# Second mixer: attention score products over all 128 rows, with half-zero keys, in place of 64 rows each

## The reference, cut to what matters

```python
def chunked_relpos_attention(q, k, v, q_gain, k_gain, rel_bias):
    q = rms_norm_2(q, q_gain)
    k = rms_norm_2(k, k_gain)
    ...
    s = jnp.einsum('bnqhd,bnkhd->bhnqk', qc, kb).astype(jnp.float32) * (HEAD_DIM ** -0.5)
    ...
    s = jnp.where(valid[None, None, :, None, :], s + bias[None, :, None], NEG_INF)
```

## Time and profile before

| | us |
|---|---|
| median of three runs | 2283.86 |
| span of the profiled execution, first to last instruction | 2283.2 |
| around the span (median less span) | 0.66 |
| TensorE matmul busy | 2079.1 (91%) |
| TensorE weight loads busy | 1764.9 (77%) |
| VectorE busy | 1232.4 (54%) |
| ScalarE busy | 854.6 (37%) |
| GpSimd busy | 498.0 (22%) |
| second mixer's attention steps 0 to 31 | 1705.5 to 1850.7 |

### The profile page before, as it was taken

How to read it: one execution, slowest core, us unless ns; L and a number is a source line. 1 busy time by engine, 2 the same in 40 slices (tenths; PEclk the granted TensorE clock), 3 DMA queues, 4 the chain that set the end, 5 groups by cost and what they waited for, 6 DMA issues and landing times. The chain is left out here.

```text
span 2283.2 us, 30308 instructions
## 1 busy us (share of the span) xinstructions
PE 2079.1 (91%) x11592; PEld 1764.9 (77%) x11592; DVE 1232.4 (54%) x2338; ACT 854.6 (37%) x1402; POOL 498.0 (22%) x339
## 2 busy tenths in 40 slices
PE   6988898899999999798989999998799999789984
PEld 6887777788888788786768888887797778777773
DVE  3676453544454447745554544448952233478885
ACT  4444433421222344343332222224224452257772
POOL 2654321000000146432110000004453335110001
PEclk9999988999999999898989999999899999799997
DMA  4111100412221111110132212207445533489995
GB/s 154 56 56 38 37 29 19 175 64 102 110 110 55 42 57 56 38 38 28 38 120 111 101 65 110 110 1 178 63 128 175 153 128 121 151 320 401 406 391 211
DMA packets 61627, 270.95 MB, mean 119 GB/s; under 512 B 15040, under 2 KB 19904, under 8 KB 37056
## 3 DMA queue, kind: packets, MB, share of 16 engines
q1 hardware_dynamic: 52864, 237.84, 30.0%
q10 hardware_dynamic: 6048, 22.02, 2.5%
q0 software_dynamic: 2592, 9.44, 1.1%
HBM read 244.14 MB, written 37.19 MB: 123 GB/s over the span
## 5 line engine op out<-in xcount | busy, mean ns | idle before, releaser
L1241 PE MATMUL fill_ps<-w_hi,h_hi 128*128 128x256 f32 (+1 forms) x704 | 214.2, 304 | 13.9 <-ACT values L866 5.2
L1241 PE MATMUL fill_ps<-w_hi,h_lo 128*128 128x256 f32 (+1 forms) x704 | 204.7, 291 | 0.0
L1241 PE MATMUL fill_ps<-w_lo,h_hi 128*128 128x256 f32 (+1 forms) x704 | 204.2, 290 | 0.0
L795 POOL TENSOR_TENSOR w_lo<-w_raw,w_hi 128x1024 fp32r<-128x1024 f32 x60 | 151.8, 2540 | 194.3 <-ACT w_hi L858 193.6
L516 DVE TENSOR_TENSOR ffn_silu<-ffn_silu,ffn_up 128x512 f32<-128x512 f32 x44 | 30.2, 687 | 285.5 <-ACT ffn_silu L474 285.5
L322 POOL TENSOR_SCALAR norm_ss<-norm_ss 128x1 f32<-128x1 f32 x24 | 4.9, 203 | 798.8 <-ACT ffn_raw_d L316 738.2
L1241 PEld LDWEIGHTS fill_ps<-w_hi,h_hi 128*128 128x128 f32 x704 | 141.8, 201 | 27.0 <-issue 16.1
L1702 POOL TENSOR_TENSOR w_lo<-w_raw,w_hi 128x1024 fp32r<-128x1024 f32 x48 | 126.1, 2643 | 165.2 <-ACT w_hi L1787 165.2
L528 DVE TENSOR_TENSOR x<-ffn_down,x 128x512 f32<-128x512 f32 x176 | 119.1, 689 | 71.2 <-PE ffn_down L590 70.4
L1321 PEld LDWEIGHTS o_ps<-values,prob_t 128*128 128x128 f32 x800 | 111.6, 201 | 57.5 <-DVE prob_t L1100 46.3
L575 PE MATMUL ffn_up<-h_hi,w_hi 128*128 128x512 f32 x384 | 152.1, 396 | 3.7 <-PEq L772 3.7
(11 more groups left out here) (444 smaller groups left out, 5639.6 us busy)
## 6 DMA issues: line engine op xcount, KB each, us to landing
moe_raw_gu<-in_w_e_gu SPq DMA_DIRECT2D x46, 1024.0 KB, 11.9
w_raw<-in_w_mix SPq DMA_DIRECT2D x28, 1024.0 KB, 4.9
w_raw<-in_w_two SPq DMA_DIRECT2D x23, 1024.0 KB, 5.0
moe_raw_d<-in_w_e_down SPq DMA_DIRECT2D x23, 1024.0 KB, 8.3
w_raw<-in_w_gate SPq DMA_DIRECT2D x22, 1024.0 KB, 5.6
w_raw<-in_w_up SPq DMA_DIRECT2D x22, 1024.0 KB, 6.5
ffn_raw_d<-in_w_down SPq DMA_DIRECT2D x22, 1024.0 KB, 4.9
moe_in<-in_zero SPq DMA_DIRECT2D x23, 512.0 KB, 7.5
```

What stands on the lines that cost most here:

```text
L795: nc.gpsimd.tensor_tensor(w_lo[s][:, cols], w_raw[s][:, cols], w_hi[s][:, cols].bitcast(F32), ALU.subtract).then_inc(lo_done, 1)
L1241: last = nc.tensor.matmul(b[:, 0:cols], aw[:, k, t * P:(t + 1) * P], ww[:, k, 0:cols], start=k == 0 and n == 0, stop=k == KD - 1 and n == 2)
```

## The change

Score products take all 128 partitions. The queries of both heads of a pair are then the stationary operand, so the keys must be zero where the other head lies. For an even head the key unit itself gets zeros on partitions 64 to 127: its buffer is zeroed (`memset`, for units 1 and 3), and later only partitions 0 to 63 are written. For an odd head GpSimd makes a separate pair of tiles, `odd_keys`: the turned keys multiplied by a column `odd_row` that is 0 on partitions 0 to 63 and 1 on 64 to 127 (three operations on 128x512 for each pair of heads, in `keys_of_odd`). They stand in GpSimd's queue behind unit 1 and at the start of steps 8, 16 and 24. The space comes from the unused half of `rel_bias`. Three semaphores are added.

```diff
+        odd_row = core.sb("odd_row", [P, 1], ctx=st)
-        rel_bias = core.sb("rel_bias", [P, 4 * SEQ], ctx=st)
+        rel_bias = core.sb("rel_bias", [P, 2 * SEQ], ctx=st)
+        odd_buf = core.sb("odd_keys", [P, 2 * SEQ], F32R, st)
...
                     s = u % 4
-                    nc.gpsimd.tensor_copy(u_hi[s], unit_in[u % 2]).then_inc(unit_hi, 1)
+                    if u in (1, 3):
+                        nc.gpsimd.memset(units[s].bitcast(F32), 0.0).then_inc(padded, 1)
+                        pool.wait_ge(padded, 2 + (u + 1) // 2)
+                    rows = EVEN if u % 2 else slice(0, P)
+                    nc.gpsimd.tensor_copy(u_hi[s][rows], unit_in[u % 2][rows]).then_inc(unit_hi, 1)
                     pool.wait_ge(unit_hi, u + 1)
-                    nc.gpsimd.tensor_tensor(u_lo[s], unit_in[u % 2], u_hi[s].bitcast(F32), ALU.subtract).then_inc(unit_lo, 1)
+                    nc.gpsimd.tensor_tensor(u_lo[s][rows], unit_in[u % 2][rows], u_hi[s][rows].bitcast(F32), ALU.subtract).then_inc(unit_lo, 1)
+
+                def keys_of_odd(m):
+                    if m:
+                        pool.wait_ge(scored, 2 * TB * m)
+                    else:
+                        pool.wait_ge(padded, 3)
+                    hi, lo, src = odd_keys[0], odd_keys[1], unit_in[1]
+                    nc.gpsimd.tensor_scalar(hi, src, odd_row[:], None, ALU.mult).then_inc(odd_hi, 1)
+                    pool.wait_ge(odd_hi, 2 * m + 1)
+                    nc.gpsimd.tensor_tensor(lo, src, hi.bitcast(F32), ALU.subtract).then_inc(odd_hi, 1)
+                    pool.wait_ge(odd_hi, 2 * m + 2)
+                    nc.gpsimd.tensor_scalar(lo, lo.bitcast(F32), odd_row[:], None, ALU.mult).then_inc(odd_lo, 1)
...
+                nc.gpsimd.memset(odd_row[:], 1.0).then_inc(padded, 1)
+                pool.wait_ge(padded, 1)
+                nc.gpsimd.memset(odd_row[EVEN], 0.0).then_inc(padded, 1)
...
                 unit(0)
                 unit(1)
+                keys_of_odd(0)
...
                 for n in range(REL_LAST + 1):
+                    if n % (2 * TB) == 0 and 0 < n < REL_STEPS:
+                        keys_of_odd(n // (2 * TB))
...
                     if u >= 2:
                         act.wait_ge(unit_lo, u - 1)
+                        if u % 2:
+                            act.wait_ge(odd_lo, u // 2)
...
                     qs, ks = a // 2 * 2 % 4, (a // 2 * 2 + 1) % 4
-                    width, cols, rows = (i + 1) * P, slice(i * P, (i + 1) * P), slice(HEAD * (a % 2), HEAD * (a % 2 + 1))
+                    width, cols = (i + 1) * P, slice(i * P, (i + 1) * P)
                     if i == 0:
                         pe.wait_ge(unit_lo, a // 2 * 2 + 2)
+                        pe.wait_ge(padded, 3 if a < 2 else 4)
+                        if a % 2:
+                            pe.wait_ge(odd_lo, a // 2 + 1)
+                    k_hi, k_lo = odd_keys if a % 2 else (u_hi[ks], u_lo[ks])
                     s = s_ps[n % 3][:, 0:width]
-                    nc.tensor.matmul(s, u_hi[qs][rows, cols], u_hi[ks][rows, 0:width], start=True, stop=False)
-                    nc.tensor.matmul(s, u_lo[qs][rows, cols], u_hi[ks][rows, 0:width], start=False, stop=False)
-                    nc.tensor.matmul(s, u_hi[qs][rows, cols], u_lo[ks][rows, 0:width], start=False, stop=True).then_inc(scored, 1)
+                    nc.tensor.matmul(s, u_hi[qs][:, cols], k_hi[:, 0:width], start=True, stop=False)
+                    nc.tensor.matmul(s, u_lo[qs][:, cols], k_hi[:, 0:width], start=False, stop=False)
+                    nc.tensor.matmul(s, u_hi[qs][:, cols], k_lo[:, 0:width], start=False, stop=True).then_inc(scored, 1)
```

More of the change, by code:

```diff
@@ L1517, in second_mixer @@
         u_lo = [u[:, SEQ:2 * SEQ] for u in units]
+        odd_keys = [odd_buf[:, SEQ * n:SEQ * (n + 1)] for n in range(2)]
+        EVEN, ODD = slice(0, HEAD), slice(HEAD, P)
         prob = [probs[:, P * (i * (i + 1) // 2):P * ((i + 1) * (i + 2) // 2)] for i in range(TB)]
@@ L1555, in second_mixer @@
         unit_turned, unit_out, unit_hi, unit_lo = (sem(n) for n in ("unit_turned", "unit_out", "unit_hi", "unit_lo"))
+        padded, odd_hi, odd_lo = sem("padded"), sem("odd_hi"), sem("odd_lo")
         bias_done, scored, maxed, exped, turned = (sem(n) for n in ("bias_done", "scored", "maxed", "exped", "turned"))
```

## The result

The changed kernel takes **2270.72 us** (median, 2268.58 to 2271.32), the kernel before 2284.04 us beside it (2283.59 to 2285.89). The ratio is 0.9933 [0.9919, 0.9947]: 13.3 us faster, where 11.7 was forecast. The profiled spans are 2269.5 us after and 2283.2 before, 13.7 apart. (In the runs that have both on record the time is 1.7 to 1.9 us longer than the span of the same execution, 2271.32 and 2269.5 here; the 0.66 us given for before compares the span of one execution with the median of others.) In the lines of after, the score's three products are L2402 to L2404 (L2369 to L2371 before), the dense product is L2292 (L2263), the transpose L2415 (L2382).

The account below looks back on a forecast made before the run. TensorE's queue was taken as the bound; 5.34 + 0.73 + 2.88 + 2.73 + 0.30 = 12.0 us, less step 14's 0.39, plus 0.15 for step 15, gave 11.7: 2283.86 - 11.7 = 2272.2 us, range 2268 to 2277.5.

Parts of the forecast that it names:

- the crossings: Changes between 64-row scores and 128-row products in second-mixer steps 0 to 31; removing them saves 12.0 us, about 0.39 a step.
- The bound: Second mixer's attention, steps 0 to 31: TensorE's queue sets the pace, and the whole gain is carried to the end.
- Entry, inside, exit, behind: Savings before the score, within it, after its third product, and after the first dense product: 5.34, 0.73, 2.88, 2.73 + 0.30 us.
- Step 14: Before the 1.83 us wait for ScalarE's exponential: its 0.39 us saving is lost because that wait grows by it.
- Step 15 and the clock: Step 15 runs at the lower clock, where the same losses take up to twice as long; 0.15 us added.
- GpSimd's work: Zeroings and `keys_of_odd` all covered: multiplication 0.67 us (1.29 at most), `keys_of_odd` 2.6 us (3.9 at most).
- The slower rival: GpSimd late, TensorE waiting for `odd_lo` at steps 12, 20 and 28; some 15 us slower, 2299 us; chance 0.03.
- the rows are not the cause: Rival: rows not the cause, or the change brings no full-row behaviour; gain 0 to 1 us, 2283 to 2284; chance 0.04.
- only the way out is mended: Rival: the entry into the scores keeps its 5.25 us price; gain 6.4 us, 2277.4 us; chance 0.07.
- Full-row loads not prefetched: Rival: the scores' 96 weight loads stand bare at 0.19 us each; 18 us more, 2302 us; chance 0.01.

Follow-up runs that it names:

- e11_mask_first: Changed kernel with one move in GpSimd's queue: head 0's bias masked before the low parts of weight chunk 10, not behind them; 2274.05 us, single run.
- e1_rows64: Changed kernel with the three score products back on 64 rows, keeping its zeroed keys, waits and GpSimd work; 2281.95 us, ratio 0.9999.
- e9_changed_again: The changed kernel run once more, unedited; 2268.98 us, ratio 0.9929.
- e2_rows_only: Kernel before with the second mixer's score products over all 128 rows, nothing zeroed, so scores include the other head's product; 2266.52 us, ratio 0.9936.
- e4_double_odd: Changed kernel with GpSimd's three operations for the odd heads' keys done twice each time; 2272.58 us, ratio 0.9953.
- e5_rows66: Changed kernel with even heads' score products on 66 rows, odd heads' on all 128; 2271.21 us, single run.
- e6_first_dsa: Changed kernel plus the same change for the last six heads (64-row scores) in both layers of the first mixer; 2242.97 us, ratio 0.9811.
- e3_alternate: Changed kernel with first and third score products on 64 rows and the second on all 128; 2296.44 us, ratio 1.0069.
- e7_first_all: e6_first_dsa plus full-row keys for five of the eight 32-row softmaxes in each layer of the first mixer; 2245.3 us, ratio 0.9825.

## Why the prediction was right

The forecast held: 11.7 us predicted, 13.3 measured, 2270.72 us inside its own range. The mechanism is shown, by undoing the rows alone, by doing them alone, and by adding crossings. That the number came so near is partly luck: the crossings were put at 11.6 us (12.0 less step 14's) and gave some 10.7, the clock was put at 0.15 and gave some 1.6, and about 1 us more lies outside the stage. Term by term:

- **The bound.** Right. TensorE's queue is full in both stages. The saving runs through to the end as far as can be told: behind the stage the changed kernel's own two profiles (437.4 and 434.0 us) lie on both sides of before (436.3).
- **Entry, inside, exit, behind.** Right in kind and nearly in size: transposes to first score 0.13 to 0.15 with two transposes, exits 0.23 to 0.24 at 512 columns. A step saves 0.345 us in steps 1 to 13 (4.14 / 12) and 0.377 in steps 16 to 31 (5.66 / 15), where 0.39 stood. Two things are missing. Behind a score of 128 columns the second dense product starts 0.28 to 0.29 us after the first and not 0.23 (0.05 in each of five steps; in the other three the turned unit stands between). The 66-row steps of the first mixer already had this: 0.17 us there behind a 128-column score, 0.12 behind the others. And step 1's saving is lost at step 2, where the changed kernel waits for 0.23 us (no such wait before); `e11_mask_first` shows that this is the order of GpSimd's work:

```profile
1703.07 0.33 PE L2402 MATMUL bank<-units 128*128 128x128 f32 x1 [1.17 <-ACT x L1913]
1710.18 0.33 PE L2415 MATMUL bank<-const,probs 128*128 128x128 f32 x1 [0.23 <-ACT probs L1868]
1765.36 0.44 PE L2415 MATMUL bank<-const,probs 128*128 128x128 f32 x2 [2.27 <-ACT probs L1868]
```

- **Step 14.** Right: the wait of 1.83 us has become 2.27, which takes back one step's saving, as said.
- **Step 15 and the clock.** Too small. I added 0.15 us for the slow stretch behind that wait. Steps 13 to 16 save 2.31 us; three steps' saving less the longer wait is 3 x 0.39 - 0.44 = 0.73, so 1.6 come from elsewhere. At the lower level TensorE runs for 6.8 us before and for 3.4 after, and 3.4 us less at half speed is 1.7. It is 6.8 in `e1_rows64` too, and 3.4 in after, in its repeat `e9_changed_again` and in four more kernels with full rows (`e2_rows_only`, `e4_double_odd`, `e5_rows66`, `e6_first_dsa`); but `e3_alternate` has 3.4 as well, with the most crossings, and `e11_mask_first` and `e7_first_all` have none, the second with the changed kernel's own second mixer. So I read it as tied to how the events fall there, not to the crossings as such; whether the change itself shortened it is open. Before, then the undone rows, then after:

```profile
1772.00:1780.00 8.00, 7.69 (x22) 5.45 (x22) 1.54 (x6) 1.11 (x5) 1.21 (x2) 0.57 0.77 262
```

```profile
1772.00:1780.00 8.00, 7.62 (x22) 5.46 (x22) 1.54 (x6) 1.15 (x5) 5.68 (x5) 0.57 0.82 262
```

```profile
1766.00:1770.00 4.00, 4.00 (x13) 3.10 (x12) 1.54 (x6) 0.00 (x0) 3.49 (x4) 0.58 0.78 265
1770.00:1774.00 4.00, 4.00 (x23) 3.45 (x22) 0.40 (x3) 3.03 (x7) 1.57 (x2) 0.99 0.81 279
```

- **GpSimd's work.** Covered, as said, but mis-sized: the multiplication by a column takes 1.57 us, over my 0.67 and over my upper bound of 1.29 too. `keys_of_odd` is 4.7 us, above the "3.9 at most". The bound rested on the dearest operation with two tiles, and a multiplication that reads one tile is dearer than it. The cover I named at step 8, 5.7 us, still held it.
- **The slower rival.** Its price was bounded wrongly. It was to decide only at 21 us for `keys_of_odd`, at TensorE's wait for the keys. The other sentence of the prediction, that the weights' low parts would suffer first, was nearer: free at 9.4 us, 25 us lost in the stage at 18.7. It decides between them, and for the low parts (10.9 us) and the masked bias (9.3), hardly for the keys (0.33).
- **The rivals that the rows are not the cause, and that only the way out is mended**: refuted by the undone rows, and by the entry of 0.15 us. **Full-row loads not prefetched**: refuted by the load lines above; full-row products follow each other at 0.23 us with their loads ahead. "TensorE: Matmul & The Clock Gate" of the Trainium skill, Part 3, says in one place that a load overlaps running products only when the row group differs, which is against these rows, and in another that a load to the background weight buffer can be pulled ahead too, which they fit.

So of the 13.3 us, some 10.7 are the crossings, some 1.6 the shorter stretch at the lower level (the change's or not), and the rest, some 1, lies within what one kernel's runs differ by.

## What to carry to other kernels

Look at the distances from start to start where products with few rows stand among products with all rows: each crossing costs about 0.2 us here, and zeros in the unused rows take it away at no price on TensorE, since a product over 128 rows takes as long as one over 64 (0.23 us at 512 columns). It pays where TensorE's queue sets the pace; in `e7_first_all`, where TensorE also waits for VectorE's copies, nothing more was gained. An engine that pays for the zeros is covered by how far ahead its products are made, and not only by its idle time before the next one.

## What the runs showed of the hardware

- 66-row products next to 128-row ones cost as full ones, `e5_rows66`; a group of 32- or 64-row ones costs a crossing on either side (third score to dense product 0.32 to 0.33 us in place of 0.23).
- GpSimd, in the changed kernel: multiplication of 128x512 by a column 1.57 us, subtraction of two tiles 1.28, cast mostly 0.61 (0.67 on the mean in the earlier trace rows). On 64 partitions the cast takes 0.61 and the subtraction 1.27: half the partitions save nothing.
- The stage repeats within 0.2 us in the six profiles of kernels with full-row scores that spend 3.4 us of it at the lower level (129.09 to 129.31 us), while `e7_first_all`, which spends none there, takes 127.50. The whole times of the kernel before, 0.6 us apart in its first three runs, span 11 us in a set of 17 (2275.99 to 2287.24). In the profiles of kernels with the same work for TensorE outside the stage, its first score starts between 1700.5 and 1705.6 us, and from its last score to the end it takes 434.0 to 441.9 us (431.6 in `e2_rows_only`, which computes other values). There the time at the lower level goes along (62.5 us in the shortest, 75.3 in the longest); ahead of it, not visibly (at 153.6 us ahead of 1540 us the first score starts at 1704.48, at 129.7 us at 1705.46). A stage's length, cut at the same events and read with its time at the lower level, tells far smaller effects than the time of the whole.
